# Head norms taken in between the attention units, convolution taps moved late, the softplus high part made on Pool

## The reference

```python
a = rmsnorm(h, g_mix)
cb, cc, cu, q, k, v = split(a @ w_in)                 # 6 x 512 columns
y = causal_conv3(cc * cu, conv_w)                      # 3 taps per channel
conv_out = head_rmsnorm(cb * y, g_conv_out)            # mean of squares over 64 channels
# stick breaking attention, 8 heads of 64, key j < query i only
z = q @ k.T / 8
log_keep = log_sigmoid(-z)                             # = -softplus(z)
suffix = sum of log_keep over the keys between j and i
attn = (exp(log_sigmoid(z) + suffix)) @ v
attn = head_rmsnorm(attn, g_attn_out)
h = h + concat(conv_out, attn) @ w_out
```

## Time and profile before

| | us |
|---|---|
| median of 3 runs | 3151.84 |
| lowest, highest | 3146.09, 3160.88 |
| the profiled execution: own time | 3155.82 |
| its span, first to last instruction | 3154.0 |
| busy: TensorE 91%, VectorE 50%, ScalarE 26%, Pool 23% | |

### The profile page before, as it was taken

One profiled execution on the slowest core, in us unless ns is written; L12 is line 12 of the kernel. 1 busy time (PEld: TensorE's weight loads), 2 busy tenths in 40 slices (PEclk: granted clock), 3 DMA queues, 4 the chain that ended last, 5 costly groups with the idle time before them and its releaser, 6 DMA issues.

```text
span 3154.0 us, 31385 instructions
## 1 busy us (share of the span) xinstructions
PE 2873.8 (91%) x12566; PEld 2220.4 (70%) x12566; DVE 1579.7 (50%) x1534; ACT 828.7 (26%) x946; POOL 735.0 (23%) x396
## 2 busy tenths in 40 slices
PE   7989999889999999899769999977899999999986
PEld 6866666667777777787537777754688888888765
DVE  5534556456746737637645665663332222222264
ACT  2522222041201301201244665564210001111031
POOL 2421001212131131131102111211233333333331
PEclk9988999999999999999879999998999999999998
DMA  3110001201011010110011000001111111111111
GB/s 117 48 43 20 14 13 41 74 20 41 21 41 34 27 41 27 34 47 21 21 66 34 27 27 27 34 14 67 40 47 47 47 47 47 47 47 60 47 34 66
DMA packets 34759, 127.50 MB, mean 40 GB/s; under 512 B 3856, under 2 KB 3984, under 8 KB 34640
## 3 DMA queue, kind: packets, MB, share of 16 engines
q1 hardware_dynamic: 28224, 102.77, 9.8%
q10 hardware_dynamic: 6416, 23.06, 1.9%
HBM read 117.43 MB, written 8.39 MB: 40 GB/s over the span
## 4 chain that ended last, share of the span: by engine, by line
PE 80%; DVE 13%; ACT 4%; issue 2%; DMA 1%; DVEq 0%; ACTq 0%; POOL 0%; POOLq 0%
PE PS L471 61%; PE PS L712 2%; PE PS L561 2%; PE PS L593 2%; PE PS L634 2%; DVE norm_t L1578 1%; PE PS L580 1%; PE PS L714 1%; PE PS L718 1%; PE PS L700 1%; PE PS L826 1%; DVE XL L1571 1%; DVE mla_rc L1491 1%; PE PS L854 1%; PE PS L843 1%
## 5 line engine op out<-in xcount | busy, mean ns | idle before, releaser
L427 POOL CAST w_hi<-w_stage 128x1024 fp32r<-128x1024 f32 x196 | 208.2, 1062 | 2356.0 <-PE PS L471 2067.0
L471 PE MATMUL PS<-XH,w_hi 128*128 128x512 f32 x2176 | 694.6, 401 | 54.2 <-DVE XL L1571 29.3
L471 PE MATMUL PS<-XH,w_lo 128*128 128x512 f32 x2176 | 679.6, 394 | 0.0
L471 PE MATMUL PS<-XL,w_hi 128*128 128x512 f32 x2176 | 679.2, 394 | 0.0
L429 POOL TENSOR_TENSOR w_lo<-w_stage,w_hi 128x1024 fp32r<-128x1024 f32 x196 | 526.7, 2687 | 15.7
L471 PEld LDWEIGHTS PS<-XH,w_hi 128*128 128x128 f32 x2176 | 403.3, 190 | 155.9 <-issue 50.4
L471 PEld LDWEIGHTS PS<-XH,w_lo 128*128 128x128 f32 x2176 | 413.6, 190 | 88.7
L471 PEld LDWEIGHTS PS<-XL,w_hi 128*128 128x128 f32 x2176 | 412.9, 190 | 88.9
L471 PE MATMUL PS<-ffn_u_hi,w_hi 128*128 128x512 f32 x512 | 161.2, 396 | 9.4 <-ACT ffn_t L1301 7.9
L1301 ACT ACTIVATE ffn_t<-PS 128x1024 f32<-128x1024 f32 x32 | 32.8, 1026 | 512.0 <-PE PS L471 512.0
L471 PE MATMUL PS<-ffn_u_hi,w_lo 128*128 128x512 f32 x512 | 160.6, 395 | 0.0
(11 more groups left out here) (328 smaller groups left out, 4027.7 us busy)
## 6 DMA issues: line engine op xcount, KB each, us to landing
w_stage<-w SPq DMA_DIRECT2D x196, 512.0 KB, 3.2
H<-x_t ACTq DMA_DIRECT2D x4, 1024.0 KB, 11.4
x_again<-x_t ACTq DMA_DIRECT2D x8, 512.0 KB, 3.2
h_kept<-H ACTq DMA_DIRECT2D x8, 512.0 KB, 2.8
h_again<-h_kept ACTq DMA_DIRECT2D x4, 1024.0 KB, 8.0
out_t<-norm_t ACTq DMA_DIRECT2D x8, 512.0 KB, 2.6
x_again<-p_t ACTq DMA_DIRECT2D x1, 1024.0 KB, 6.9
CN<-consts ACTq DMA_DIRECT2D x1, 576.0 KB, 5.2
```

Source lines behind the costliest of these rows:

```text
L427: nc.gpsimd.tensor_copy(w_hi[:, slot, :, :], w_stage[:, slot, :, :]).then_inc(s_w_hi, 1)
L471: mm = nc.tensor.matmul(outs[:, half, :], wt[:, slot, k, :], a[:, k - first, half * HB:(half + 1) * HB], start=(k == whole[0] and wt is w_ ...
```

## The change

- The order of slabs, SB_ORDER, puts cb of unit m behind k of unit m+1; SB_FILL gives unit 0 eight tiles fewer and unit 3 eight more.
- Seven of the eight head norms are made within the units. HEAD_STEPS says where TensorE makes the sums of which tile: tile 4 at unit 1 step 2, tile 0 at unit 1 step 5, tiles 5 and 1 in unit 2, tiles 6, 2 and 3 in unit 3 (steps 2, 5, 12). The squares stand in one buffer (where the turned v stands, too) and the sums in PSUM pair 6/7, in the order of s_bank. ScalarE squares in the same step (for step 2: in step 1) and takes logarithm and exponential in the next; VectorE scales in place, behind the softplus low part of that next step. High and low parts are made when all input slabs are done, as they overwrite the input's.
- The first output slab takes its tiles in the order HEAD_ORDER, with the sums of tile 7 behind the third.
- VectorE makes the first tap directly from PSUM ahead of the product, and the two other taps behind the softplus low part of the step.
- Pool makes the high part of the softplus and splits a slab where the order says that TensorE finishes the slab two places before.
- The loads of h have four semaphores.

```diff
-SB_ORDER = [("v", 0), ("q", 0), ("k", 0), ("cc", 0), ("cu", 0), ("cb", 0), ("v", 1), ...
+SB_ORDER = [("v", 0), ("q", 0), ("k", 0), ("cc", 0), ("cu", 0), ("v", 1), ("q", 1), ("k", 1),
+            ("cb", 0), ("cc", 1), ("cu", 1), ("v", 2), ("q", 2), ("k", 2),
+            ("cb", 1), ("cc", 2), ("cu", 2), ("v", 3), ("q", 3), ("k", 3), ("cb", 2), ("cc", 3), ("cu", 3), ("cb", 3)]
-SB_BANK_USE = [key for key in SB_ORDER if key[0] != "k"]
+HEAD_STEPS = {(1, 2): 4, (1, 5): 0, (2, 2): 5, (2, 5): 1, (3, 2): 6, (3, 5): 2, (3, 12): 3}
+HEAD_TURNS = [4, 0, 5, 1, 6, 2, 3, 7]
+HEAD_ORDER = [0, 1, 2, 4, 5, 6, 3, 7]
+HEAD_AFTER = {("cb", 0): 4, ("cc", 1): 0, ("cb", 1): 5, ("cc", 2): 1, ("cb", 2): 6, ("cc", 3): 2, ("cb", 3): 3}
+SB_BANK_USE = [use for key in SB_ORDER if key[0] != "k" for use in (key, ("head", HEAD_AFTER.get(key))) if use[1] is not None] + [("head", 7)]
 SB_FILL = [
-    [(2, 1), (2, 1), (2, 1), (3, 0), (2, 1), (1, 2), (2, 1), (3, 1), (3, 1), (3, 1), (3, 1), (3, 0), (2, 2), (2, 2)],   # units 0, 1, 2
-    [(2, 1), (2, 1), (2, 0), (1, 1), (1, 0), (2, 0), (1, 1), (1, 1), (1, 1), (2, 0), (1, 0), (2, 0), (0, 0), (0, 0)]]
+    [(2, 1), (2, 0), (3, 0), (2, 0), (2, 0), (2, 0), (2, 1), (2, 1), (2, 1), (1, 2), (2, 1), (3, 0), (2, 2), (2, 2)],
+    [(2, 1), (2, 1), (2, 0), (3, 1), (2, 1), (1, 0), (3, 1), (4, 0), (3, 1), (4, 0), (3, 1), (4, 0), (2, 2), (2, 2)],   # units 1, 2
+    [(2, 1), (2, 1), (2, 0), (2, 1), (2, 0), (3, 0), (2, 1), (2, 1), (2, 0), (2, 1), (2, 1), (2, 0), (0, 0), (0, 0)]]
...
+            for m in range(4):                                        # Pool
+                for step in range(SB_STEPS):
+                    if step < NU:
+                        q0, T = SB_WIDE[step], NU * m + step
+                        pool.wait_ge(s_sp, T + 1)
+                        nc.gpsimd.tensor_copy(SPH[:, T % 3, :, q0:HB], SPF[:, T % 3, :, q0:HB]).then_inc(s_sph, 1)
+                    for key in sb_finished(m, step, 0) + sb_finished(m, step, 1):
+                        next_slab(SB_AT[key] + 2)
...
+            def head_sums(k):                                         # TensorE
+                pe.wait_ge(s_hq, HEAD_TURNS.index(k) + 1)
+                pe.wait_ge(s_bank, sb_bank_turn(("head", k)))
+                for half in range(2):
+                    mm = nc.tensor.matmul(PS[:, 6 + half, :], CN[:, C_BLK, :], HQ[:, half * HB:(half + 1) * HB], start=True, stop=True)
+                mm.then_inc(s_hs, 1)
...
+                    if (m, step) in HEAD_STEPS:                       # between values and late tiles
+                        head_sums(HEAD_STEPS[m, step])
...
+            for i, k in enumerate(HEAD_ORDER):                        # first output slab
+                if i == 3:
+                    head_sums(7)
+                pe.wait_ge(s_hl, i + 1)
+                mm = product(pair(N_OUT2 % 2), N_OUT2, XH, XL, [k], 0, HEAD_ORDER)
...
+            def head_root(k):                                         # ScalarE
+                act.wait_ge(s_hs, HEAD_TURNS.index(k) + 1)
+                inverse_root(HQ[:, :], flat(3), 64, EPS6, s_bank, sb_bank_turn(("head", k)), s_hr)
...
+                    if (m, step + 1) in HEAD_STEPS and step == 1:     # behind Abs and the slab's copy, ahead of Exp
+                        head_square(HEAD_STEPS[m, step + 1])
+                    if (m, step) in HEAD_STEPS and step != 2:
+                        head_square(HEAD_STEPS[m, step])
+                    if (m, step - 1) in HEAD_STEPS:
+                        head_root(HEAD_STEPS[m, step - 1])
...
-                        nc.scalar.activation(SPH[:, T % 3, :, q0:HB], l, ACT.Copy).then_inc(s_sph, 1)
...
+                    if step == NU and m == 3:                         # behind the high part of the weights
+                        head_hi(0)
+                        head_hi(1)
...
+            for j in range(4):
+                act.dma_start(H2[:, 2 * j:2 * j + 2, :], h_kept[2 * j:2 * j + 2, :, :]...).then_inc(s_h2[j], 16)
+            head_hi(2)
+            head_square(7)
+            for i in range(3, 7):
+                head_hi(i)
+            head_root(7)
+            head_hi(7)
...
                 elif kind == "cu":                                    # VectorE
-                    v.tensor_tensor(CC[:, :], flat(3), CC[:, :], ALU.mult).then_inc(s_bank, 1)
-                    cc(v.tensor_scalar(y, CC[:, :], col("c2_w", 8 + m), None, ALU.mult)); cc.wait()
-                    for d in (1, 2):
-                        cc(v.scalar_tensor_tensor(...)); cc.wait()
+                    cc(v.scalar_tensor_tensor(out=CONV[:, m, :], in0=flat(3), scalar=col("c2_w", 8 + m), in1=CC[:, :],
+                                              op0=ALU.mult, op1=ALU.mult))
+                    v.tensor_tensor(CC[:, :], flat(3), CC[:, :], ALU.mult).then_inc(s_bank, 1)
...
+                    for key in sb_finished(m, step, 0):               # behind the softplus low part
+                        if key[0] == "cu":
+                            sb_taps(key[1])
+                    if (m, step - 1) in HEAD_STEPS:
+                        head_scale(HEAD_STEPS[m, step - 1])
+                    if m == 3 and step == NU:
+                        ...
+                        head_lo(0)
+                        head_lo(1)
```

More of the change, by code:

```diff
@@ L339, in program @@
         s_hk = sem("h_kept")
-        s_h2 = sem("h_again_loaded")
+        s_h2 = [sem(f"h_again_loaded{j}") for j in range(4)]
         s_mask = sem("sb_masks_made")
@@ L430, in split, with next_slab @@
                                         w_hi[:, slot, :, :].bitcast(F32), ALU.subtract).then_inc(s_w_ready, 1)
-            for n in range(NSLAB):
+            def next_slab(n):
                 if n >= 2:
@@ L435, in _ @@
                 split(n, n % 2, 16 * (n // 2) + 16, n + 1)
+            for n in range(N_IN2 + 5):
+                next_slab(n)
+            for m in range(4):
[6 more added lines that the diff above has]
+                        next_slab(SB_AT[key] + 2)
+            for n in range(N_OUT2 + 2, NSLAB):
+                next_slab(n)
         class Tiles:
@@ L890, in _ @@
             assert progress[0] == 8 * len(SB_ORDER)
-            for k in range(8):
-                pe.wait_ge(s_hq, k + 1)
-                if k >= 2:
-                    pe.wait_ge(s_hv, k - 1)
-                for half in range(2):
-                    mm = nc.tensor.matmul(PS[:, 4 + 2 * (k % 2) + half, :], CN[:, C_BLK, :], HQ[:, k % 2, half * HB:(half + 1) * HB],
-                                          start=True, stop=True)
-                mm.then_inc(s_hs, 1)
-            stream(N_OUT2, 8, XH, XL, (s_hl, 0))
+            take(N_OUT2)
+            for i, k in enumerate(HEAD_ORDER):
[3 more added lines that the diff above has]
+                mm = product(pair(N_OUT2 % 2), N_OUT2, XH, XL, [k], 0, HEAD_ORDER)
+            mm.then_inc(s_slab, 1)
+            for n in range(N_OUT2 + 1, N_OUT2 + 8):
+                take(n)
+                product(pair(n % 2), n, XH, XL).then_inc(s_slab, 1)
             norm_pe_streamed(mlp)
@@ L1211, in sb_copies @@
                 if kind == "v":
+                    if m >= 2:
+                        act.wait_ge(s_ht, 2 * (m - 1))
                     nc.scalar.activation(VT[:, :], flat(3), ACT.Copy).then_inc(s_bank, 1)
@@ L1232, in low_parts, with head_source, head_square, head_hi @@
                 nc.scalar.activation(OS[0:64, :], PS[64:128, 5, :], ACT.Copy).then_inc(s_os, 1)
+            def head_source(k):
+                return CONV[:, k, :] if k < 4 else ATT[:, k - 4, :]
+            def head_square(k):
+                if k >= 4:
+                    act.wait_ge(s_at, 4 * (k - 4) + 4)
+                else:
+                    act.wait_ge(s_bank, sb_bank_turn(("cb", k)) + 1)
+                if HEAD_TURNS.index(k):
+                    act.wait_ge(s_ht, HEAD_TURNS.index(k))
+                nc.scalar.activation(HQ[:, :], head_source(k), ACT.Square).then_inc(s_hq, 1)
+            def head_root(k):
+                act.wait_ge(s_hs, HEAD_TURNS.index(k) + 1)
+                inverse_root(HQ[:, :], flat(3), 64, EPS6, s_bank, sb_bank_turn(("head", k)), s_hr)
+            def head_hi(i):
+                k = HEAD_ORDER[i]
+                act.wait_ge(s_slab, N_OUT2)
+                act.wait_ge(s_ht, HEAD_TURNS.index(k) + 1)
+                nc.scalar.activation(XH[:, k, :], head_source(k), ACT.Copy).then_inc(s_hh, 1)
             for key in SB_ORDER[:3]:
@@ L1256, in _ @@
                         nc.scalar.activation(a, a, ACT.Exp).then_inc(s_w, 1)
-                    if step < NU:
-                        act.wait_ge(s_sp, T + 1)
-                        nc.scalar.activation(SPH[:, T % 3, :, q0:HB], l, ACT.Copy).then_inc(s_sph, 1)
                     if 1 <= step <= NU:
@@ L1778, in sb_lows, with sb_taps @@
                     cc(v.memset(SM[:, 3, 0:1], 0.0))
+            def sb_taps(m):
+                y = CONV[:, m, :]
```

(15 more changed lines are left out.)

58 lines of the change are left out of this document (12 added, 46 removed), and 3 rows, old and new, of the table SB_FILL.

## The result

The changed kernel takes **3193.25 us** (median of 4 runs, 3182.93 to 3197.25) beside 3148.97 for the kernel before (4 runs). The ratio is 1.0127, 95% interval 1.0103 to 1.0151: 1.3% slower, outside the range I gave (3120 to 3168) and on the other side of zero from the sum. The profiled execution has a span of 3193.8 us and an own time of 3195.67.

A forecast was written before the change was run, and what follows sets the result against it. TensorE was taken to bound units 0 to 2, a VectorE and ScalarE chain unit 3. Terms summed to -14.7 us; clock +8.5 and slow start +1 made -5 from 3151.84: 3147 us, range 3120 to 3168.

The forecast's parts named there:

- Tail: Last value product to end of first output slab: 55.4 us become 16.5 as seven head norms leave, -38.9 us.
- low parts in step 12: VectorE makes low parts 0 and 1 ahead of the last weight low part: last value product 3.5 us later.
- Fill: Eight tiles (10.9 us) go from unit 0 to unit 3; unit 0 102.4, units 1 and 2 122.6, unit 3 110.3.
- Bank waits: Units 1 to 3: TensorE waits for ScalarE's logarithm before a slab's first tile, 3.5 us after step 2, 4.0 after step 5.
- High part on Pool: Softplus high part in all units: Pool cast of 1.04 us replaces ScalarE copy of 1.09, no gain, taken as 0.
- Rival C: Pool splits collide with VectorE low parts, 2.3 us in each of nine slabs of units 0 and 3: 3168 us, chance 0.12.
- Clock: Granted clock drops at six new waits, some hidden in unit 3: +8.5 us; slow start of first output slab +1.
- Taps: Slab cu with late taps: carry late by 2.0 us, value product waits 1.3; next to nothing saved in idle.
- the dear row: Unit 2's granted clock of 0.79 over 16 us around a wait: 3.4 us lost, 20 us for six waits.
- B: Clock falls at every bank wait, 3.4 us each, and waits are 5.3 us: about +14, 3166 us, chance 0.10.
- rival A: Bank waits vanish, costing 1 us each instead of 3.75, and their clock drops go: about -28, 3124 us, chance 0.30.

The follow-up runs named there:

- e6: Changed kernel with softplus high part on ScalarE, head-norm logarithm in its sums' step, tail low parts 0 and 1 behind the last weight low part: 3139.45 us.
- e9: Changed kernel with splits held until the next step's weight low part is done and the head-norm logarithm in the step of its sums: 3116.04 us, ratio 0.9894.
- e8: Changed kernel with each split inside the units held until VectorE has made the next step's weight low part: 3147.59 us, ratio 0.9985.
- e1: Changed kernel with the softplus high part back on ScalarE and Pool only splitting slabs: 3163.79 us, ratio 1.0042.
- e2: Kernel before with only the softplus high part moved to Pool, between its splits: 3168.81 us, ratio 1.0062.
- e11: Kernel before with the softplus high part on Pool and the splits held behind the weight low part: 3134.51 us, ratio 0.9961.
- e13: Kernel before with only the splits held behind the weight low part, high part still on ScalarE: 3144.45 us, ratio 0.9985.
- e7: Same as e6, but slab cu in the old order, product and all taps ahead of the carry's difference: 3145.09 us, ratio 0.9987.

## Why the prediction was wrong

- *Tail, -38.9*: right in its place, 15.9 us against 16.5. But the terms as I wrote them add up to 18.5, if the third tile ends at 9.5 us and the block sums follow; they give 16.5 only if the block sums end at 9.5. In the trace they end at 8.2, and from there to the end it takes 7.8 where I had 7.0. The low parts in step 12 stand as said (3.5 us), but e6 shows that moving them wins only 1.
- *Fill*: near, 1 to 4 us low in each unit. In e9, with 3.2 us of bank waits and the low parts free of collisions, units 0 to 3 take 106.0, 116.4, 116.4 and 105.5; the forecast less its bank waits (7.5 a unit) is 102.4, 115.1, 115.1 and about 103. Unit 0 is 3.6 us over, with no norm in it; no run takes that apart.
- *Bank waits, 3.5 and 4.0*: right in place, releaser and count; 3.85 and 5.32 measured. The upper bound that I gave, 5.3 "where VectorE is behind by what an overlapping weight split costs it", was the value in step 6, and splits that hold VectorE up were the reason: in e8, where the low parts are free of them, the six waits are 3.50 and 4.51 us, in e1, where splits start freely, 4.66 and up to 5.70.
- *"High part on Pool ... I take 0"*: **the step that failed.** I priced the copy (1.04 for 1.09), which was right, and the wait of the split, but not when the split now starts. Rival C had the mechanism and even the price: 2.3 us a slab, measured 0.8 + 1.1 in the pair above and more where the rest of the subtraction is longer. The sign that I had named for it, softplus low parts of over 2 us, is there (2.03), and I had given it 0.12. I let it count in nine slabs of units 0 and 3 only, as "in units 1 and 2 TensorE covers it". Yet TensorE's waits for the weight low part, 8 with 10.0 us over the four units before, are 15 with 29.9 us now; e1 gains 8.1 and 7.9 us in units 1 and 2, more than the 7.5 and 4.4 in units 0 and 3. Worth: 28 us by e1, 16 to 20 by e2.
- My argument against C, that splits of the kernel before "collide in the same manner", was true (e11, e13: they cost it 5 us or more) and no argument: it is what they hit that counts. There it was mostly the softplus and one tap instruction, 12 us of lengthening at full width; here it is both low parts, which the suffix sums and the value product wait for, and 28 us.
- *Clock, +8.5 and +1*: **mis-sized.** The missing clock of the units rose by 31 us and TensorE's busy time over the whole stretch by 18.0; filling the six waits alone gives back 12.5 to 20, 2.1 to 3.3 each. I had taken the mean of two rows, 1.7 per wait; the clock fell at all six, so the dear row (3.4, 0.79 in the earlier trace rows) was nearer.
- *Taps*: 2.19 for 2.0 at the carry, right; 3.98 for 1.3 at the value product, since two instructions there collided. "Next to nothing in idle" was wrong: in e6 and e7 late taps save 14 us at the carry and 6 to 8 in the time.
- *The rivals as exclusive cases*: B (waits of 5.3, a clock drop at each) and C came true together: splits that hold VectorE up also make B's longer waits. B was 19 us above the forecast, C 21; both on top of 3147 give 3187, near the 3193 measured. That nearness is partly luck: I had C's 21 us in units 0 and 3 alone, where e1 gains 12, and nothing in units 1 and 2, where it gains 16. For rival A I wrote 3124; its own terms give 3122.

By the Trainium skill's rule ("TensorE: Matmul & The Clock Gate", section "HAM oscillation — how this bites in real kernels") repeated waits make each following burst start cold. The trace of the changed kernel agrees in kind, with 1.19 us for 0.70 behind each of the six waits. Priced by my dearest row the term would have been 20 us, the upper end of the 12.5 to 20 measured; my 8.5 lies below both.

What stays open: the 3.6 us of unit 0, and whether the clock's price is nearer 12.5 or 20. And the copy's own gain beside late splits (e11 against e13) is 3 us in the sums and 8 in the ratios, whose intervals overlap, so it may be nothing.

## What to carry to other kernels

When an instruction is moved to Pool's queue, ask what starts right behind it, and on which VectorE instruction that falls. Here work of Pool and work of VectorE released by the same event collided in 18 of 21 splits, and on the instructions that TensorE waits for. Released by TensorE, as in the kernel before, splits collided too, with less than half of the lengthening (12 us at full width against 28). One wait, `s_wl` ahead of the split, was worth 40 us. Likewise a reader that frees a bank belongs in its own step, ahead of anything that waits for the next step's data (38 us for moving one call). And where waits, blocks and the clock feed each other, don't treat them as exclusive rivals: a case in which they come together needs its own price and its own chance.

## What the runs showed of the hardware

- A weight cast of 1.04 us on Pool that began 0.09 us before a VectorE low part held it up for 0.8 us (2.03 for 1.22). With the subtraction of 2.4 to 3.3 us it is anything up to 2.2 us (3.38 for 1.22), by how much of it is left. VectorE's copy of 1.21 us from PSUM ran through the same subtraction unchanged.
- The tap multiply reads one SBUF tensor and is blocked too: 754 ns left alone (e13), 2.75 us beside a subtraction of 2.39. Two inputs aren't needed for a block; alone it is also faster than the two-input instructions of its size (1.22).
- Pool pays as well: its subtraction averaged some 2450 ns in the units before and 2936 after.

```profile
L430 POOL TENSOR_TENSOR w_lo<-w_stage,w_hi 128x1024 fp32r<-128x1024 f32 x22 | 64.6, 2936 | 1.8
```

- Pool's cast of 128x1024 takes 1041 ns, as fast as ScalarE's copy of the same tile (1.07 in the earlier trace rows).
- 114 matmuls of no use, laid into idle waits of 4 to 5 us, made the kernel faster by 12.5 us by the sum and 20 by the ratios; the granted clock rose from 0.92 to 0.96 over the 530 us, and the matmuls of use kept TensorE busy for 12.9 us less.
